# The last pair's small product made at the end and read from the accumulators, the residual added in the output by an adding DMA

## What is computed

```python
def per_layer_embed(x, p_i, norm_g, w_gate, w_proj):
    gate = jax.nn.sigmoid((rms_norm(x, norm_g) @ w_gate).astype(jnp.float32))
    return x + (p_i @ w_proj) * gate.astype(x.dtype)

# x: (1, 256, 4096); p_i: (1, 256, 256); w_gate: (4096, 4096); w_proj: (256, 4096)
```

## Time and profile before

| | us |
|---|---|
| median of three runs | 1643.84 |
| the profiled execution | 1644.54 |
| its span, first to last instruction | 1642.8 |
| TensorE busy | 1634.7 |
| VectorE busy | 1347.0 |
| ScalarE busy | 959.5 |
| GpSimd busy | 29.4 |

### The profile page before, as it was taken

The page is one execution under the profiler, slowest core; times in us unless marked ns, Lnnn a source line. Parts: engine busy times, 40 slices in busy tenths (PEclk is TensorE's granted clock), DMA queues, the critical chain, the costliest instruction groups (busy, mean ns, idle before and its releaser), DMA issues.

```text
span 1642.8 us, 22407 instructions
## 1 busy us (share of the span) xinstructions
PE 1634.7 (100%) x7974; PEld 1380.5 (84%) x7974; DVE 1347.0 (82%) x1651; ACT 959.5 (58%) x1260; POOL 29.4 (2%) x27
## 2 busy tenths in 40 slices
PE   9999999999999999999999999999999999999998
PEld 7888888888888888888888888888888888888887
DVE  6778877868777786878778779989889978989898
ACT  6654555646555555655555656656566756566664
POOL 1010000000000000000000000000000000000000
PEclk9999999999999999999999999999999999999999
DMA  8766665656556565655656567766666575757664
GB/s 307 216 184 190 196 190 155 206 159 183 179 160 197 154 204 158 188 172 163 190 160 208 162 193 248 248 207 240 208 234 215 196 247 187 257 197 241 227 212 160
DMA packets 134374, 328.43 MB, mean 200 GB/s; under 512 B 10656, under 2 KB 15264, under 8 KB 134304
## 3 DMA queue, kind: packets, MB, share of 16 engines
q1 hardware_dynamic: 133168, 326.93, 63.3%
q10 hardware_dynamic: 1136, 0.57, 0.1%
HBM read 319.08 MB, written 8.39 MB: 199 GB/s over the span
## 4 chain that ended last, share of the span: by engine, by line
PE 99%; DMA 1%; DVE 0%; ACT 0%; SPq 0%; issue 0%
PE bank L1954 13%; PE bank L1956 13%; PE bank L1957 13%; PE bank L1725 13%; PE bank L1726 13%; PE bank L1727 13%; PE bank L1765 3%; PE bank L1764 3%; PE bank L1763 3%; PE bank L1799 2%; PE bank L1801 2%; PE bank L1800 2%; PE bank L1860 1%; PE bank L1780 1%; DMA raw<-in_w_in_dram 1%; PE bank L1772 1%
## 5 line engine op out<-in xcount | busy, mean ns | idle before, releaser
L1053 DVE TENSOR_TENSOR w_lo<-raw,w_hi 128x1024 fp32r<-128x1024 f32 x266 | 324.2, 1222 | 134.9 <-ACT w_hi L576 133.9
L576 ACT ACTIVATE w_hi<-raw 128x1024 fp32r<-128x1024 f32 x266 | 280.0, 1056 | 193.5 <-PE bank L1727 160.3
L1725 PE MATMUL bank<-w_lo,aT_hi 128*128 128x512 f32 x944 | 370.5, 393 | 0.0
L1726 PE MATMUL bank<-w_hi,aT_hi 128*128 128x512 f32 x944 | 368.2, 390 | 0.0
L1727 PE MATMUL bank<-w_hi,aT_lo 128*128 128x512 f32 x944 | 367.7, 389 | 0.0
L1954 PE MATMUL bank<-w_lo,aT_hi 128*128 128x512 f32 x668 | 260.6, 390 | 0.0
L1957 PE MATMUL bank<-w_hi,aT_lo 128*128 128x512 f32 x668 | 259.9, 389 | 0.0
L1956 PE MATMUL bank<-w_hi,aT_hi 128*128 128x512 f32 x668 | 259.9, 389 | 0.0
L718 ACT ACTIVATE w_hi<-raw 128x1024 fp32r<-128x1024 f32 (+1 forms) x126 | 132.7, 1057 | 150.7 <-PE bank L1957 133.3
L1727 PEld LDWEIGHTS bank<-w_hi,aT_lo 128*128 128x128 f32 x944 | 177.2, 188 | 37.5
L1725 PEld LDWEIGHTS bank<-w_lo,aT_hi 128*128 128x128 f32 x944 | 177.6, 188 | 34.2
(11 more groups left out here) (373 smaller groups left out, 2738.2 us busy)
## 6 DMA issues: line engine op xcount, KB each, us to landing
raw<-in_w_in_dram SPq DMA_DIRECT2D x318, 512.0 KB, 3.6
raw<-in_w_out_dram SPq DMA_DIRECT2D x100, 512.0 KB, 4.3
raw<-in_w_gate_dram SPq DMA_DIRECT2D x90, 512.0 KB, 4.9
stage<-in_w_gate_dram SPq DMA_DIRECT2D x38, 512.0 KB, 5.1
stage<-in_w_out_dram SPq DMA_DIRECT2D x28, 512.0 KB, 5.1
out_dram<-arena SPq DMA_DIRECT2D x7, 1024.0 KB, 5.6
arena<-in_x_dram SPq DMA_DIRECT2D x4, 1024.0 KB, 8.4
stage<-in_xT_dram SPq DMA_DIRECT2D x7, 512.0 KB, 6.0
```

What stands on the lines that cost most here:

```text
L576: nc.scalar.activation(w_hi[:, i % RING, :], raw[:, i % RING, :], ACT.Copy).then_inc(hi_done, 1)
L1053: nc.vector.tensor_tensor(w_lo[:, i % RING, :], raw[:, i % RING, :], w_hi[:, i % RING, :].bitcast(F32), ALU.subtract).then_inc(lo_done, 1)
L1725: nc.tensor.matmul(outs[t][:, :], ahi, wlo, start=first and jj == 0, stop=False)
L1726: nc.tensor.matmul(outs[t][:, :], ahi, whi, start=False, stop=False)
```

## The change

The product of the last pair is made in `last_projection`, behind the last tile quad, part by part, into banks 4, 5, 6, 7 and 4 again (`last_bank`). `last_product` reads these banks, so `pj_copy` of pair 3 is gone. Both blocks' weights must then stand at once, so block b = 1 gets buffers of its own (`wp_last_hi`, `wp_last_lo`, weight slot 2); it is split at the end of the pair. The fifth part uses bank 4 again and waits for the first part's product.

The residual is not loaded back any more but for one tile. Behind the products of a pair, GpSimd issues a DMA that adds the pair to x1 in `out` (1 MB, three of them); behind each of the first three parts of the last pair one of 256 KB. The last tile's two halves get their x1 from SBUF (`x1_last`, loaded once), an add on VectorE and a store by SP as before. `outputs`, `load_x1r` and `store` are gone. At the end SP waits for the six adding DMAs and the two stores.

```diff
+            def load_x1_last():
...
+                sp.dma_start(x1_last, out[P:2 * P, (2 * m + 1) * N:(2 * m + 2) * N]).then_inc(x1r_in, 16)
...
             for k, (t, b, lo, hi) in enumerate(LAST_PARTS):
-                sp.wait_ge(out_ready, 4 * m + k + 1)
+                if k < 3:
+                    continue
+                sp.wait_ge(out_ready, k - 2)
                 col = (2 * m + b) * N
                 sp.dma_start(out[t * P:(t + 1) * P, col + lo:col + hi], tile(t, b)[:, lo:hi]).then_inc(out_stored, 16)
-            sp.wait_ge(out_stored, 16 * (PAIRS - 1) + 80)
+            sp.wait_ge(out_added, 16 * (PAIRS + 2))
+            sp.wait_ge(out_stored, 32)
...
+            pool.wait_ge(spilled, 16 * PAIRS)
+            for m in range(PAIRS - 1):
+                pool.wait_ge(gated, 4 * m + 4)
+                pool.dma_start(out[:, m * 2 * N:(m + 1) * 2 * N].rearrange("(t q) n -> q t n", q=P), cc,
+                               accum_op=ALU.add).then_inc(out_added, 16)
+            m = PAIRS - 1
+            for k, (t, b, lo, hi) in enumerate(LAST_PARTS[:3]):
+                pool.wait_ge(gated, 4 * m + k + 1)
+                pool.dma_start(out[t * P:(t + 1) * P, (2 * m + b) * N:(2 * m + b + 1) * N], tile(t, b),
+                               accum_op=ALU.add).then_inc(out_added, 16)
...
                 else:
-                    act.wait_ge(out_stored, 16 * m)
+                    act.wait_ge(out_added, 16 * m)
...
+                elif (m, b) == (PAIRS - 1, 1):
+                    act.wait_ge(pe_half, ends(pair_quads(GATE, m)[LAST_FAST], 3))
+                    nc.scalar.activation(wp_last_hi, wp_raw[b], ACT.Copy).then_inc(wp_top, 1)
...
                                     gate_sigmoids(m - 1)
-                                    wp_hi_part(m, 1)
+                                    if m < PAIRS - 1:
+                                        wp_hi_part(m, 1)
...
-                                elif (pos, h) in ((2, 1), (2, 3)):
-                                    pj_copy(m, h // 2)
+                                elif (pos, h) == (QUADS - 1, 1):
+                                    wp_hi_part(m, 1)
...
                                 elif (pos, h) == ((1, 1) if m == PAIRS - 1 else (2, 0)):
-                                    wp_lo_part(m, 1)
+                                    if m < PAIRS - 1:
+                                        wp_lo_part(m, 1)
                                     gate_products(m - 1)
-                                elif (m, pos, h) in ((1, 4, 0), (2, 4, 0), (3, 3, 1)):
-                                    outputs(m - 1, 0)
-                                elif (m, pos, h) in ((1, 8, 1), (2, 8, 1), (3, 9, 1)):
-                                    outputs(m - 1, 1)
...
+            wp_lo_part(PAIRS - 1, 1)
+            for k in range(len(LAST_PARTS)):
+                last_sum_of(k)
+            for k in range(len(LAST_PARTS)):
+                last_product(k)
+                if k >= 3:
+                    last_output(k)
...
+            def last_projection():
...
+                for k, (t, b, lo, hi) in enumerate(LAST_PARTS):
+                    whi, wlo = (wp_hi, wp_lo) if b == 0 else (wp_last_hi, wp_last_lo)
+                    pe.wait_ge(wp_split, 2 * (PAIRS - 1) + b + 1)
+                    if k == len(LAST_PARTS) - 1:
+                        pe.wait_ge(gated, 4 * (PAIRS - 1) + 1)
+                    for jj in range(PLE_T):
+                        ps = last_bank(k)[:, lo:hi]
...
+                        nc.tensor.matmul(ps, phi, wlo[:, jj, lo:hi], start=begins, stop=False)
+                        nc.tensor.matmul(ps, phi, whi[:, jj, lo:hi], start=False, stop=False)
+                        last = nc.tensor.matmul(ps, plo, whi[:, jj, lo:hi], start=False, stop=closes)
+                    last.then_inc(last_proj, 1)
...
-                            elif s == GATE:
+                            elif s == GATE and m < PAIRS - 1:
                                 if (pos, h) == (0, 1):
                                     projection(m, 0)
                                 elif (pos, h) == (1, 1):
                                     projection(m, 1)
+
+            last_projection()
```

More of the change, by code:

```diff
@@ L262, in encoder_layer @@
         u_gate = T[:, 0, :]
+        wp_last_hi, wp_last_lo = (e[2].rearrange("q (a n) -> q a n", a=PLE_T) for e in (slot_hi, slot_lo))
         wp_raw = [stage4[:, 2:4, 1, :], at(9472, 1024).rearrange("q (a n) -> q a n", a=PLE_T)]
@@ L288, in tile, with last_bank @@
             return cc[:, t, b * N:(b + 1) * N]
+        def last_bank(k):
+            return bank[(4, 5, 6, 7, 4)[k]]
         def pj(t, b):
             return stage4[:, 2 * t + b, 0, :]
-        def x1r(m, t, b):
-            return T[:, b, :] if (m, t) == (PAIRS - 1, 1) else stage4[:, b, 1, :]
+        x1_last = stage4[:, 0, 1, :]
         def raw_set(k):
@@ L472, in load_wp @@
                 sp.dma_start(dst, src).then_inc(wp_in[b], 16)
[L474 to L491, removed]
+            def load_x1_last():
+                sp.wait_ge(s1_done, 2)
+                sp.wait_ge(spilled, 16 * PAIRS)
+                m = PAIRS - 1
+                sp.dma_start(x1_last, out[P:2 * P, (2 * m + 1) * N:(2 * m + 2) * N]).then_inc(x1r_in, 16)
             for k, q in enumerate(loads):
@@ L507, in _ @@
                         load_wp(0, b, wp0_raw[b])
[L508 to L511, removed]
-                elif n == 13 and s == GATE:
[L513 to L517, removed]
+                elif n == 13 and s == GATE and m < PAIRS - 1:
+                    if m == 0:
+                        sp.wait_ge(s1_done, 2)
+                    sp.wait_ge(wp_split, 2 * m + 2)
+                    for b in range(2):
+                        load_wp(m + 1, b, wp_raw[b])
+                elif n == 13 and s == GATE:
+                    load_x1_last()
             m = PAIRS - 1
-            load_x1r(m, 1)
             for k, (t, b, lo, hi) in enumerate(LAST_PARTS):
-                sp.wait_ge(out_ready, 4 * m + k + 1)
+                if k < 3:
+                    continue
+                sp.wait_ge(out_ready, k - 2)
                 col = (2 * m + b) * N
                 sp.dma_start(out[t * P:(t + 1) * P, col + lo:col + hi], tile(t, b)[:, lo:hi]).then_inc(out_stored, 16)
-            sp.wait_ge(out_stored, 16 * (PAIRS - 1) + 80)
+            sp.wait_ge(out_added, 16 * (PAIRS + 2))
+            sp.wait_ge(out_stored, 32)
         @block.gpsimd
@@ L1582, in gate_products @@
                     nc.vector.tensor_tensor(tile(t, b), pj(t, b), tile(t, b), ALU.mult).then_inc(gated, 1)
[L1584 to L1589, removed]
             def wp_lo_part(m, b):
@@ L1633, in last_product @@
                 t, b, lo, hi = LAST_PARTS[k]
-                if k == 0:
-                    dve.wait_ge(pj_out, 2 * PAIRS)
+                dve.wait_ge(last_proj, k + 1)
                 dve.wait_ge(gate_ready, 4 * (PAIRS - 1) + k + 1)
                 part = tile(t, b)[:, lo:hi]
-                nc.vector.tensor_tensor(part, pj(t, b)[:, lo:hi], part, ALU.mult).then_inc(gated, 1)
+                nc.vector.tensor_tensor(part, last_bank(k)[:, lo:hi], part, ALU.mult).then_inc(gated, 1)
             def last_output(k):
                 t, b, lo, hi = LAST_PARTS[k]
-                if k == 0:
-                    dve.wait_ge(x1r_in, 32 * PAIRS)
+                if k == 3:
+                    dve.wait_ge(x1r_in, 16)
                 dve.wait_ge(gated, 4 * (PAIRS - 1) + k + 1)
                 part = tile(t, b)[:, lo:hi]
-                nc.vector.tensor_tensor(part, x1r(PAIRS - 1, t, b)[:, lo:hi], part, ALU.add).then_inc(out_ready, 1)
+                nc.vector.tensor_tensor(part, x1_last[:, lo:hi], part, ALU.add).then_inc(out_ready, 1)
             for s in (OUT, GATE):
@@ L2031, in projection @@
                 last.then_inc(proj_ps, 1)
+            def last_projection():
+                pe.wait_ge(p1_out, PAIRS + 1)
+                pe.wait_ge(evac, evac_base(GATE, PAIRS - 1) + 4)
+                for k, (t, b, lo, hi) in enumerate(LAST_PARTS):
[5 more added lines that the diff above has]
+                        ps = last_bank(k)[:, lo:hi]
+                        phi, plo = pT_hi[jj][:, t * P:(t + 1) * P], pT_lo[jj][:, t * P:(t + 1) * P]
+                        begins, closes = jj == 0, jj == PLE_T - 1
+                        nc.tensor.matmul(ps, phi, wlo[:, jj, lo:hi], start=begins, stop=False)
+                        nc.tensor.matmul(ps, phi, whi[:, jj, lo:hi], start=False, stop=False)
+                        last = nc.tensor.matmul(ps, plo, whi[:, jj, lo:hi], start=False, stop=closes)
+                    last.then_inc(last_proj, 1)
             for s in (OUT, GATE):
```

23 lines of the change are left out of this document (7 added, 16 removed).

## The result

The changed kernel takes 1646.30 us (median of 20 runs, 1645.42 to 1648.37), the kernel before 1644.13 (20 runs). The ratio is 1.0013, 95% interval [1.0007, 1.0019]: 2.2 us more, where 0.2 was predicted. The time is inside the range of 1642.2 to 1647.0, but above the 1643.2 to 1645.3 that the forecast itself had. It is slower, but by less than the 0.2% that the prediction counted as a change.

The account below looks back on a forecast made before the run. TensorE was taken to bound the kernel, VectorE second. Span 1642.8 + 0.08 (small product) + 1.27 (stall) - 1.15 (shorter end) = 1643.0; 0.2 us added to the median 1643.84 gave 1644.0 us, range 1642.2 to 1647.0.

Parts of the forecast that it names:

- The stall: Head of last pair, first seven-product quad: TensorE waits for VectorE's weights at two units, 1.27 us, bounds 0 and 3.4.
- The smooth rival: Last pair: no stall and a short adding DMA, everything up by 1.27 us, time 1642.2; chance 0.12.
- the fourth: Last pair: VectorE, not TensorE, sets the pace, the 5.44 us are not returned, time 1648.2; chance 0.03.
- The product at the end: Behind the tile quads: small product runs without gaps to 1639.17, VectorE's last add ends at 1640.25 against 1640.62.
- The adding DMA: End of kernel: third tile's DMA issued by GpSimd at 1638.6, lands 4.0 us later, then 0.4 us to span end.
- The sum: Whole kernel: 1642.8 + 0.08 + 1.27 - 1.15 gives a span of 1643.0.
- The bounds of the prediction: Landing time of a 256 KB adding DMA: from 2.0 us, a plain store, to 5.8, store behind a read.
- The store behind it: End of kernel: SP's last 128 KB land after 1.7 us, a path giving span 1642.4, ahead of the adding DMA.
- The second rival: End: three adding DMAs queue on GpSimd's issue; chance 0.20 of over 1.5 us, 0.09 of over 3.1 us.
- The third rival: End: GpSimd cannot issue while VectorE works, third adding DMA starts at 1640.25, time 1645.7; chance 0.05.
- The other pairs: Pairs 1 and 2: residual adds, loads and stores go away, TensorE waited for none, costed at nothing; 1 MB DMAs hidden.

Follow-up runs that it names:

- c: Changed kernel with pair 2's four gate products spread over four later units at the head of the last pair; 1644.78 us, ratio 1.0006 to the kernel before.
- a: Changed kernel without adding DMAs in the last pair: VectorE adds the residual of all five parts, SP stores them; 1643.87 us, ratio 1.0000.
- g: Changed kernel with c's spread gate products and only the last pair's first part added by DMA, VectorE adding the other four; 1642.42 us, again 1642.83.
- e: Changed kernel with the last pair's three 256 KB GpSimd DMAs as plain stores, residual left out there; 1643.77 us, ratio 1.0002.

## Why the prediction was right in its order and short in its size

**The stall: right.** 0.82 + 0.45 = 1.27 us was forecast, at the first two units of the first seven-product quad and nowhere else; the trace has 0.85 + 0.45 there and no other wait. With 0.38 added the first unit starts at 1561.28 (forecast 1561.36) and the second at 1562.42 (1562.49); the gate products start at 1558.14 (about 1558.2). Run c shows that it costs what it lasts, 1.30 us. The smooth rival, with no stall, is refuted by the same rows; it would have needed VectorE further ahead than the 0.94 us of idle time in rows 5 allowed. So is the fourth, that VectorE paces the whole pair: the tile quads end at 1633.34 + 0.38 = 1633.72, forecast 1633.65.

**The product at the end: right.** No gap from 1633.18 to the last matmul, no wait for a bank, a sigmoid or the split of block 1. The third product ends at 1637.46 + 0.69 + 0.38 = 1638.53 (forecast 1638.55), the last add at 1639.91 + 0.38 = 1640.29 (1640.25). So VectorE's last add ends 0.33 us earlier than before (1640.62), as forecast. That this becomes 0.4 us of time where no adding DMA ends later is not shown: in a, which has none at the end, VectorE makes three more adds, its last one ends 7.1 us behind the tile quads instead of 6.6, and the time is that of the kernel before.

**The adding DMA: the step that failed.** The sum put the issue of the third at 1638.6 and its landing 4.0 us behind, at 1642.6. Measured, with 0.38 added: GpSimd begins to issue at 1638.83, 0.30 us after the product, and the DMA lands 5.65 us after that, at 1644.48, together 1.88 us late. The 4.0 was not a bad value for one adding DMA: the first lands after 4.1 us, g's after 3.95 and, run again, 4.3. What the sum left out is that the three are on the same 16 DMA engines: they come 1.36 us apart and each holds the engines for 1.88 us, so each finds the one before it still there. That gives the direction, not the whole size: such a queue alone adds 0.5 us to the second and 1.0 to the third, and they took 1.2 and 1.55 more than the first. Where the other 0.5 to 0.7 us come from is open. The bounds of the prediction were drawn for a single DMA, and the third came near the upper one, 5.8 us.

**The store behind it: not in the sum at all.** SP's last 128 KB were given the 1.7 us of rows 10, since the sum compared two paths as if each had the engines to itself. They took 4.5 us and landed 0.38 us after the adding DMA, where the prediction had them landing first. The 1.88 us of the adding DMA and these 0.38 make 2.26 us, which is what the span (1644.9 + 0.38 = 1645.28, forecast 1643.0) is over, within 0.02.

**The second rival: right in the outcome, wrong in the mechanism.** It had the three DMAs queue behind one another, by the time GpSimd needs to issue one. GpSimd needs 0.86 to 0.90 us, less than the 1.36 between two, and is idle for 0.46 and 0.50 us ahead of the second and the third. The queue is one stage further on. The price fits what was named: 1.9 us over the forecast landing, in the part of the cases with "over 1.5 us", to which the prediction gave 0.20. That the time lies inside the range is owed to the room left for this rival and not to the sum; that another queue fell into the same room is luck.

The Trainium skill, page "DMA: Bandwidth & Descriptors", section "Anatomy of one DMA — SWDGE (gpsimd) path", gave 2.6 us as an estimate. The plain stores of e, with 2.3 us, are close to it; the adding ones, with 3.9 to 5.7, are not, and the measurement decides.

**The third rival: refuted.** GpSimd's third issue begins at 1638.45, in the middle of VectorE's run of products and adds from 1637.46 to 1639.91, and takes 0.86 us like the second, which began at 1637.09 while VectorE was idle. It is not held until the run ends.

**The other pairs: right.** The adding DMAs of 1 MB land after 11.9 us where a store took 5.6, and no row of TensorE's waits has a trace of them in the last pair, where the third of them is issued (1560.55). No wait in the trace is ended by one of them.

## What to carry to other kernels

Before a step at the very end is moved to other DMAs, add up what all of them, the stores behind them too, take of the 16 engines, and set that against the time between the first issue and the end; paths that share the engines are not to be compared as if each were alone. An adding DMA cost no time that was seen where it had time to land (the 1 MB ones, the first tile of the last pair); among the last stores VectorE's add is cheaper. Work taken off the busiest engine at one place may have been the cover for another one there: look at what that engine waits for next, and move that too, as c did.

## What the runs showed of the hardware

- A DMA that adds 256 KB to the output lands 3.9 to 4.3 us after its issue when none is ahead of it (the first or only one of each run) and up to 5.7 in a row of three; a plain one of the same size from GpSimd 2.3, from SP 2.0. In engine time it is 1.8 to 2.0 us (1.88 in the changed kernel, 1.98 for g's one, 18.0% of 11 us) against 0.69 to 0.72. Why the addition costs some 2.7 times as much, which part of it is the reading of the old values, was not tried.
- GpSimd's issue of an adding DMA of 256 KB takes 0.84 to 0.91 us, of a plain one 0.54 to 0.61.
- Stores of another queue that are issued meanwhile wait for those engines: SP's 128 KB took 4.5 us instead of 1.7 behind three adding DMAs, 2.9 behind two, 1.8 behind one that had landed or was about to (g and g again).
